# Norm 1's tiles scaled and split in turn, six unread products fewer, a third low part on GpSimd

## What is computed

```
cond = silu(c)
mod = (cond @ w_ada + b_ada).reshape(b, 6, d)
shift1, scale1, gate1, shift2, scale2, gate2 = [mod[:, i] for i in range(6)]
hn = modulate(rmsnorm(x, norm1_g), shift1, scale1)      # h * (1 + scale) + shift
proj = hn @ w_in
qa, ka, va, qi, ki, wi, qb, kb, vb, ga, gb = split(proj, offsets)
```

## Time and profile before

| | |
|---|---|
| median of 3 runs | 1447.53 us |
| lowest, highest of them | 1444.44, 1451.73 us |
| span of the profiled execution | 1450.8 us |
| TensorE matmul, busy | 1402.9 us (97%), 10406 records |
| VectorE, busy | 1097.6 us (76%) |
| ScalarE, busy | 836.6 us (58%) |
| GpSimd, busy | 358.2 us (25%) |
| chain of waits, by engine | TensorE 80%, VectorE 13%, ScalarE 4%, DMA 1%, GpSimd 1% |
| granted TensorE clock, mean | 0.988 |

### The profile page before, as it was taken

How to read it: one execution, slowest core, us unless ns; L and a number is a source line. 1 busy time by engine, 2 the same in 40 slices (tenths; PEclk the granted TensorE clock), 3 DMA queues, 4 the chain that set the end, 5 groups by cost and what they waited for, 6 DMA issues and landing times.

```text
span 1450.8 us, 25879 instructions
## 1 busy us (share of the span) xinstructions
PE 1402.9 (97%) x10406; PEld 1303.3 (90%) x10406; DVE 1097.6 (76%) x1903; ACT 836.6 (58%) x1447; POOL 358.2 (25%) x227
## 2 busy tenths in 40 slices
PE   7999999899999999999999999999999999899997
PEld 5998899799999999999988888887889899799997
DVE  6788887467889888999766666777667667787762
ACT  3554774444454577777654454465446666766651
POOL 3216101234345100000032322344322221433200
PEclk9999999999999999999999999999999999999999
DMA  9757775445655444444456666665666535275530
GB/s 383 270 187 268 248 240 176 160 150 187 187 182 162 155 151 148 148 150 148 146 188 220 196 192 193 217 191 183 190 205 244 180 115 189 81 252 177 191 116 30
DMA packets 73721, 268.24 MB, mean 185 GB/s; under 512 B 8401, under 2 KB 9730, under 8 KB 72834
## 3 DMA queue, kind: packets, MB, share of 16 engines
q1 hardware_dynamic: 71280, 256.41, 54.0%
q10 hardware_dynamic: 1426, 7.56, 1.5%
q0 software_dynamic: 896, 2.62, 0.5%
HBM read 262.88 MB, written 3.67 MB: 184 GB/s over the span
## 4 chain that ended last, share of the span: by engine, by line
PE 80%; DVE 13%; ACT 4%; DMA 1%; POOL 1%; issue 1%; DVEq 0%; ACTq 0%; POOLq 0%
PE bank L611 79%; DVE split L1834 3%; DVE ada_acc L1869 2%; DVE PR L2284 1%; DVE PR L2281 1%; ACT split L1298 1%; DMA ringb<-in_w_ada 1%; DVE PR L2289 1%; POOL H L2652 0%; DVE rT L1920 0%; PE bank L787 0%; POOL split L2625 0%; DMA vecs<-in_vecs 0%; DVE H L2373 0%; DVE PA L2085 0%
## 5 line engine op out<-in xcount | busy, mean ns | idle before, releaser
L611 PE MATMUL bank<-H,split 128*128 128x256 f32 x5928 | 736.3, 283 | 17.1 <-DVE split L1834 7.1
L611 PEld LDWEIGHTS bank<-H,split 128*128 128x128 f32 x5928 | 713.8, 190 | 24.1 <-DVE split L1834 9.4
L1298 ACT CAST split<-ringb 128x1024 fp32r<-128x1024 f32 x350 | 365.8, 1047 | 288.6 <-PE bank L611 278.4
L611 PE MATMUL bank<-split,H 128*128 128x512 f32 (+1 forms) x1728 | 390.9, 387 | 1.7 <-POOL split L2625 1.5
L2625 POOL TENSOR_TENSOR split<-ringb,split 128x1024 fp32r<-128x1024 f32 x91 | 225.4, 2478 | 670.4 <-ACT split L1298 670.4
L1834 DVE TENSOR_TENSOR split<-ringb,split 128x1024 fp32r<-128x1024 f32 x259 | 327.6, 1268 | 77.7 <-ACT split L1298 77.5
L611 PEld LDWEIGHTS bank<-split,H 128*128 128x128 f32 x1728 | 320.9, 188 | 69.8 <-POOL split L2625 2.5
L2373 DVE TENSOR_TENSOR H<-PR,H 128x256 fp32r<-128x256 f32 x128 | 137.3, 1074 | 106.3 <-ACT H L1637 106.2
L1834 DVE TENSOR_TENSOR split<-far,split 128x1024 fp32r<-128x1024 f32 x77 | 99.8, 1304 | 33.4 <-ACT split L1298 33.2
L1298 ACT CAST split<-far 128x1024 fp32r<-128x1024 f32 x89 | 92.9, 1047 | 53.2 <-PE bank L611 44.0
L1613 ACT ACTIVATE PR<-bank 128x512 f32<-128x512 f32 (+31 forms) x59 | 28.6, 486 | 75.9 <-PE bank L611 75.9
(11 more groups left out here) (298 smaller groups left out, 1265.0 us busy)
## 6 DMA issues: line engine op xcount, KB each, us to landing
ringb<-in_u SPq DMA_DIRECT2D x128, 512.0 KB, 3.6
ringb<-in_v SPq DMA_DIRECT2D x128, 512.0 KB, 4.2
ringb<-in_w_ada SPq DMA_DIRECT2D x28, 512.0 KB, 5.3
far<-in_w_up SPq DMA_DIRECT2D x26, 512.0 KB, 4.2
far<-in_w_ada SPq DMA_DIRECT2D x20, 512.0 KB, 5.1
ringb<-in_w_up SPq DMA_DIRECT2D x17, 512.0 KB, 4.9
ringb<-in_w_pq SPq DMA_DIRECT2D x16, 512.0 KB, 3.7
far<-in_w_dn SPq DMA_DIRECT2D x14, 512.0 KB, 4.0
```

Of the source, the lines that this page charges most:

```text
L611: return TE.matmul(o, l, r, start=start, stop=stop, skip_group_check=True)
L1298: S.copy(buf(m)[0], slots[P.slot[m]]).then_inc(hi_done, 1)
```

## The change

Four edits, all at the start of the program.

- `scaled` runs for tile 0, then `mod_part(2)`, then `scaled` for tile 1; from there the low tile j and the scaling of tile j+2 alternate.
- `keep_busy(8)` becomes `keep_busy(2)`.
- `w_qi`'s first two units are taken with `alone=2`: tiles 0 and 1 with unit 0 alone, then tiles 0 and 1 with unit 1, then as before.
- The low part of `w_qi`'s third unit moves from VectorE to GpSimd, ahead of its DMAs.

```diff
     def on_pool(i):
         if i in first or O0 <= i < UP0 or i >= DN6:
             return False
-        if QI0 <= i < QI0 + 2:
+        if QI0 <= i < QI0 + 3:
             return True
...
             ada_total()
-            keep_busy(8)
+            keep_busy(2)
...
             mh = normed(0)
-            lin("w_qi", 4, hk, mh, both=True)
+            lin("w_qi", 4, hk, mh, both=True, alone=2)
             one("w_ki", hk, mh)
...
             v.wait_ge(mod_done, 1)
-            scaled(range(8))
+            scaled((0,))
             mod_part(2)
+            scaled((1,))
             v.wait_ge(mod_done, 2)
             for j in range(8):
+                if j:
+                    scaled(range(j + 1, min(j + 2, 8)))
                 v.wait_ge(n_hi, j + 1)
...
             st["pos"] = P.at["w_qi", 0]
-            units(1)
+            units(2)
             fourth = P.at["w_qi", 3]
```

## The result

The changed kernel takes 1453.7 us (median of 22 runs, 1448.5 to 1457.9), the kernel before 1447.8 us in 22 runs beside them. The ratio is 1.0037, with a 95% interval of 1.0025 to 1.005: **+5.4 us, between 3.6 and 7.2**. The forecast was 1450.3 us and "within 0.5%", its range 1445.0 to 1454.0. The profiled execution took 1452.57 us, with a span of 1450.8.

The account below looks back on a forecast made before the run. TensorE was taken as the bound, through when it finishes w_qi's first block. Standing low tiles (0.7 us later) and the low clock made +2.8 us in all, other terms zero: 1447.53 + 2.8 = 1450.3 us, range 1445.0 to 1454.0.

Parts of the forecast that it names:

- upper bound: First w_qi block: with the clock back only after 5.7 us, it ends at 46.2 us, 3.4 us later.
- Low tile 0: VectorE's first low tile: issued at 33.55 us, stands behind GpSimd's second low part until 35.13, there at 35.6.
- Low tile 1 and the third low part: GpSimd's third low part runs 35.5 to 37.85 us; VectorE's tile 1, issued at 35.95, stands until 37.72.
- The clock: TensorE in the first w_qi block: 1.2 GHz for 4.6 us after products resume, back at 42.85 us.
- Its cost is in the clock: keep_busy(8) to 2 ahead of the block: frees 0.7 us at most, worth nothing here; dropping products costs through the clock.
- The DMAs at zero: GpSimd's DMAs start at 37.9 instead of 35.2 us, SyncE's load at about 37.9 instead of 40.4: zero effect.
- The end of the block: TensorE ends the first w_qi block at 45.6 us instead of 42.86, 2.8 us later.
- What held the start?: Before, unread products slowed by the clock's fall held the block's start to 37.18 us; without the fall, 36.45.
- the sum: Whole kernel: +2.8 us, bounds +0.7 and +3.4, giving a median of 1450.3 us.
- No standing still: Rival, chance 0.15: low tiles pass GpSimd's low parts, block ends at about 40.7 us, -2.1 us, 1445.4.
- Early clock: Rival, chance 0.20: VectorE stands, but the clock is back by 39 us; +0.7 to +1.1 us, 1448.4.
- Clock down for long: Rival, chance 0.04: clock stays down until 52.8 us; +7.2 us, 1454.8 and up.

Follow-up runs that it names:

- e1_psum: The changed kernel with the eight scaled tiles written to PSUM banks instead of SBUF; ratio 0.9996, -0.6 us against before.
- e3_busy8: The changed kernel with keep_busy(8) again instead of keep_busy(2); ratio 1.0016, +2.3 us against before.
- e4_only_busy2: The kernel before with keep_busy(2) instead of keep_busy(8) and nothing else changed; ratio 1.0021, +3.0 us.
- f4: The changed kernel with the third low part back on VectorE and keep_busy(8); ratio 0.9997, -0.4 us against before.
- f3: The changed kernel with scaled tiles in PSUM and keep_busy(4); 0.9976, -3.5 us against before; second run on another chip 0.997, -4.3 us.
- g4: The changed kernel with scaled tiles in PSUM, keep_busy(4) and the third low part back on VectorE; ratio 0.9988, -1.7 us against before.
- second profile of before: The kernel before run again unedited as a control; ratio 1.0005, its profiled execution 1444.77 us.
- f1: The changed kernel run again with no edit, giving its second profile; ratio 1.0036, +5.2 us against before.
- g2_busy16: The kernel before with keep_busy(16) instead of keep_busy(8); ratio 1.0027, +3.9 us.
- f2: The kernel before with only the third unit's low part moved to GpSimd; ratio 1.0008, +1.2 us.

## Why the prediction was right, and what it got wrong

The mechanism was right in its steps. The size was not: +2.8 us were forecast, with +3.4 as the upper bound, and +5.4 (3.6 to 7.2) came. The measured 1453.7 us lies 0.3 us inside the range only because the range also took in the scatter of a median, so that the number fits is in part luck.

**Low tile 0.** Forecast: issued at 33.55 us, through at 35.6. Measured: 33.05 to 35.08 us, everything ahead of it being 0.4 us earlier than in the profile of before. It stood for GpSimd's second low part as worked out.

**Low tile 1 and the third low part.** Forecast: GpSimd from 35.5, tile 1 from 35.95 to 38.2 us. Measured: GpSimd from 34.75, so it doesn't wait for tile 0 as I had it, and takes 2.54 us (2.40 in e1_psum, where nothing meets it); tile 1 from 35.39 to 37.57. The standing is 2.18 - 0.47 = 1.7 us (forecast 1.8). e1_psum takes the second SBUF input away and both stand no more: shown.

**TensorE.** Forecast: tile 0 at 35.65, a pause to 38.25. Measured: 35.22, pause to 37.62.

**The clock.** Forecast: back at 42.85 us. Measured: 42.3, and 42.7 in the second profile. e3_busy8 sizes it: with keep_busy(8) the tiles stand and the clock stays, and the products from tile 1 on take 2.0 us less than in the change (2.4 less than in its second profile). Forecast for that step, 2.8 less 0.7 = 2.1 us. The 4.6 us of low clock in it were a choice between two rows and not worked out; the two profiles have 4.7 and 5.4 us from tile 1's first product on, so hitting it is in part luck. The upper bound has a slip: 5.7 us at 1.2 GHz hold 26.8 products, the other 18.2 take 2.15 us, and the block ends at 46.1 us, +3.2 and not +3.4.

**keep_busy.** "Its cost is in the clock": e4_only_busy2 shows it on the kernel before, where the first product starts at 35.91 instead of 35.94 us and the block still ends 2.5 us later.

**alone=2** was held to be worth nothing. It has no run of its own; f4 (-0.4 us) leaves it little room for harm.

**The DMAs at zero.** GpSimd's start at 37.23 us instead of 35.20, SyncE's load into the third unit's slot at 37.31 us:

```profile
37.31 0.33 SPq L2779 DMA_DIRECT2D far<-in_w_kb  x1
```

e1_psum has the DMAs as late (37.30 us) and is not above before, and f3's kernel with them at 37.51 us in its second run is not slower (-4.3 us) than g4 with them at 34.42 us (-1.7). A cost is not seen, to within the 2 us or so that such a comparison can tell.

**The end of the block.** Forecast: 45.6 us; measured by the cast, 45.01 with a start 0.43 us earlier. In lengths, 2.8 us were forecast and 2.5 (2.9 in the second profile) came against the profile that I worked from.

**The step that was mis-sized** is the first one, "What held the start?" and with it **the sum**. The prediction took the profile of before as the kernel: unread products slow because the clock fell, the block at 37.18 us. It noted that the block would start at 36.45 us "had it not fallen", and that the profiled execution lay 3.3 us above the median; it took the 3.3 us off the time but nothing off the block. The second profile of before has no fall and a stretch 0.7 us shorter. Set against that, the term is +3.2 to +3.6 us instead of +2.8.

**What stays open: the rest of about 1 to 2 us.** The block loses 3.2 to 3.6 us, the kernel 5.4 (3.6 to 7.2). The interval's lower end would just allow for nothing behind the block, but the slope of 1.44 over the thirteen rows speaks for something. Is it the clock elsewhere? From the mean granted clock of every run I took the time spent at 1.2 GHz, 2 x (1 - clock) x time. It is 38.5 us for the change and 39.0 in f1, and 27.5, 30.4 and 29.0 us for the kernel before in the three groups. 38.7 less 29.0 us, on average, are 9.7 us more at 1.2 GHz (each of the five means has a standard error of 1 to 2 us). But the block itself accounts for 10.2 us of them in the change, against none in the better course of before and 3.4 in the other, and what they cost there, 2.0 to 2.4 us, is already in the stretch: in about half of them TensorE waited for tiles. So behind the block there is no more time at 1.2 GHz than before (9.7 - 10.2 us) if before mostly takes the better course, and 2.9 us more if it takes the other, worth 2.9 x (1 - 0.118 / 0.213) = 1.3 us. Block and clock together then explain 3.2 to 3.6 us in the one case and 2.5 to 2.9 plus 1.3 us in the other, and 1 to 2 of the 5.4 us have no cause that a run shows.

The traces show where it went in one execution each. Against the second profile of before, ScalarE's casts are 3.4 us late from 42 to 108 us, some 5 us from 130 to 1200 us, and the spans end 1450.8 - 1442.9 = 7.9 us apart. Granted clock in two stretches, all engines (PE, PEld, DVE, ACT, POOL, then PEclk), the change first:

```profile
118.00:140.00 22.00, 20.39 (x97) 16.59 (x96) 17.90 (x16) 8.91 (x12) 17.07 (x16) 0.84 0.76 260
1267.00:1271.00 4.00, 3.93 (x20) 3.93 (x21) 3.49 (x3) 2.70 (x3) 2.36 (x2) 0.59 0.68 214
```

```profile
118.00:140.00 22.00, 20.69 (x122) 17.37 (x122) 17.85 (x19) 10.98 (x15) 14.70 (x16) 0.92 0.83 280
1267.00:1271.00 4.00, 4.00 (x37) 4.00 (x36) 3.66 (x6) 3.77 (x7) 0.00 (x0) 1.00 0.89 322
```

But that profile of before has less time at 1.2 GHz than its group, 2 x (1 - 0.992) x 1444.77 = 23.1 us against 29.0, so a part of the 7.9 us is a good execution of it. Against the first profile of before the same trace ends level (both spans 1450.8 us), since that one had its own low stretches elsewhere. With two profiles a side I can't say whether a longer first block makes later falls likelier or whether four profiles fell as they did by chance. g2_busy16, made to tell a pure delay from a delay with a low clock, was too coarse.

**The rivals.** "No standing still" fell with the 2.03 and 2.18 us, and e1_psum, which makes it come true, ends the block at 8.61 us of stretch, 2.3 us under the profile that I worked from and 1.6 under the better course: its block gain of 2.1 us was about right. "Early clock" fell with the clock at 0.50 past 41 us. "Clock down for long" fell in the block (42.3 and 42.7 us, not 52.8). That the late DMAs cost the time fell in e1_psum. That the clock alone did it fell in e3_busy8, where it is not down in the block and the stretch is still 1.8 us longer than in the better course of before (1.2 without the late `w_ada` sum).

## What to carry to other kernels

When work is moved ahead in time on VectorE, look at what GpSimd does at its new place: an instruction with two SBUF inputs that met a GpSimd low part stood for the rest of it (1.5 to 1.8 us each time here), and with one operand in PSUM the meeting was free. Products that nobody reads are worth their number as long as TensorE waits for tiles, and no longer: in the kernel before, two and sixteen of them in place of eight cost 3.0 and 3.9 us. Whether four are better than two with PSUM tiles (-3.5 and -4.3 us against -0.6) is not shown: the intervals overlap, and the stretches hardly differ (8.24 and 8.69 us against 8.61). And take the profile that a sum is built on for one of several courses: if it lies off the median of its runs and shows the clock falling while TensorE still has products to run, work the sum against both courses.

## What was not expected of the hardware

One kernel takes two courses at the same place: the granted clock fell at 32.7 us among the unread products in one profile of before and stayed at 1.00 in the other, with the same sixteen records. In the two profiles of the change it fell at 32.1 and 32.4 us, while the two unread products ran or as they ended, and came back 4.7 and 5.4 us after the products had resumed behind a pause of 1.42 us; with eight unread products ahead, a pause of 1.72 us (e3) and one of 2.17 us (f2) left it at 2.4 GHz. And 1 us more of stretch went with 1.44 us more of time (standard error 0.14) at the end of this kernel, which no run explained.
